# Dense stages of a two-block transformer kernel: waits by bank and by k step where there was one wait per stage

## The chip, the cores and the metric

The kernel runs on one core of a Trainium2 chip. The metric is the time of one execution on the device, in microseconds, taken as the median of several runs.

## The reference

All values are float32. The sequence has 256 tokens, the model width is 1024, the hidden width of the feed-forward parts 2816. The first block is

```python
x = x + 0.5 * swiglu(rms_norm(x, ffn1_norm[l]), ffn1_w_in[l], ffn1_w_out[l])
h = rms_norm(x, mix_norm[l])
p_rwkv, p_q, p_k, p_v, p_gate = _split_last(h @ w_in[l], ...)
y_a = rwkv7_time_mix(p_rwkv, ...)      # a scan over 256 tokens, 16 heads of 64
y_b = dilated_attention(p_q, p_k, p_v, ...)
g_a, g_b = _split_last(jax.nn.sigmoid(p_gate + b_gate[l]), (D_MODEL, D_MODEL))
merged = g_a * (y_a @ w_proj_rwkv[l]) + g_b * (y_b @ w_proj_attn[l])
x = x + merged @ w_out[l]
x = x + 0.5 * swiglu(rms_norm(x, ffn2_norm[l]), ffn2_w_in[l], ffn2_w_out[l])
```

The second has two layers over these 256 tokens and 256 context tokens; each layer is, in short,

```python
ul, uc = _split_cols(hl @ w_in), _split_cols(hc @ w_in)
ml_l, ml_c = _mlstm_branch(ul, uc, ml_gate_b, ml_head_g)
da_l, da_c = _diff_attn_branch(ul, uc, da_lam, da_head_g, cos, sin, lam_init, need_ctx)
fn_l, fn_c = _fourier(ul[8]), _fourier(uc[8])
gm, gd, gf = jnp.split(jax.nn.sigmoid(g_pre), N_BRANCH, axis=-1)
y = gm * (ym @ w_br_ml) + gd * (yd @ w_br_da) + gf * (yf @ w_br_fn)
x = x + gate * (y @ w_out)
x = x + gate2 * ((silu(a) * b) @ w_ffn_out)     # a, b = split(h @ w_ffn_in)
```

In the last layer the context tokens are needed only as keys and values, so most products have 256 columns there and 512 in the layer before (`nq`).

## The kernel before, in words

Activations lie transposed in SBUF: 8 tiles (`KT`) of 128 features by 256 or 512 tokens. Weights come from HBM in slabs of 2 MB (`SLAB`, 32 blocks of 128 x 128) or 1.4 MB (`DOWN`, 22 blocks) into a ring of three slots. SP issues them in the order of `stage_list`, each as soon as `tile_done` says that the slab three before it has been used.

A dense stage (`Stage`, a row of `stage_list`) is one or more slabs. `project` (line 530) makes four output tiles of each slab, one in each of PSUM banks 0 to 3, each with 8 matmuls over k. When a tile is complete, `tile_done` goes up; ScalarE (`act_out`) or VectorE (`dve_out`) evicts it. `by_act` and `by_dve` say whose eviction of bank c in slab j - 1 must be over before slab j writes that bank. `project_tokens` (line 553) is the same with tokens as output rows. Banks 4 to 7 serve norms, transposes and attention.

Between stages stands `enter` (line 520): it waits until all evictions of all stages before are done, both on `act_out` and `dve_out`.

The stages that matter here:

- `ffn` (line 603): eleven `up` slabs; ScalarE puts silu of banks 0 and 1 into a buffer, VectorE multiplies with banks 2 and 3 into `hid` (22 tiles). Then eight `down` slabs, each 22 matmuls over `hid` into banks 0, 1, 2 in turn, behind an `enter`.
- `rwkv_r`, `rwkv_k`, `rwkv_v`, `rwkv_lora_in`: ScalarE evicts with line 1279, and VectorE mixes each tile with its shifted self. `rwkv_lora_out` has 24 small tiles (lines 1300 to 1304). Two gate stages follow, and then the scan, between whose steps `ada_fill` places the 12 slabs of `ada0`, in bank 7.
- `merge` (line 629) does for each of two halves a gate stage (sigmoid by ScalarE, line 1260) and a projection stage, whose tiles VectorE multiplies with the gates and, but for the first branch, adds to the sum `G2` (lines 1657 and 1658). `mix_out` and `l0_out`, `l1_out` multiply that sum with the output weights. Before them VectorE says `dve_for_pe` by a one-element memset (`say`, line 1663).
- In each layer `ml_q`, `ml_k`, `ml_v` (evictions of lines 1488, 1489, 1491), attention, `ml_o`, merge, `da_q`, `da_k` (1507, 1508), each followed by `rotate` (line 1080), which multiplies the evicted tiles with a permutation into banks 4 to 7, `da_v` (1510), attention, merge, `fn` (1537), two Fourier products, merge, output stage, `ffn`.

`norm_sums` (line 592) adds the squares of 8 tiles by matmuls with ones, each behind its own wait. All matmuls are recorded at line 515, in `matmul`.

Of the kernel before, what the change touches and what calls it, by code (L numbers as in the profile page):

```python
# [18 lines left out]
P = 128  # L19
D = 1024  # L20
KT = D // P
T = 256
# [277 lines left out]
def program(nc, x_in, ctx_in, wide_in, down_in, par_in, const_in, const1_in, const2_in, out, dbg=None):  # L300
    with ExitStack() as ctx:
# [208 lines left out]
        def _(pe):  # L510
# [19 lines left out]
            def project(st, rhs, n, kt=KT, drains=None, part=(0, 4)):  # L530
# [22 lines left out]
            def project_tokens(st, lhs, n_tok, width, groups=4):  # L553

                enter(st)
                for j in range(st.slabs):
                    arrived(st, j)
                    for q in range(n_tok):
                        if j >= 1:
# [42 lines left out]

            def ffn(name, h, width):
# [3 lines left out]
                enter(st)  # L607

                def body(j, i):
                    arrived(st, j, i)  # L610
                    b = j % SLOTS
                    if j >= SLOTS:
                        pe.wait_ge(S["dve_out"], st.dve0 + j - SLOTS + 1 + i * SLOTS)
                    for k in range(FT):
                        last = matmul(bank[b][:, 0:width], wtile(st, j, k), hid[:, k], start=k == 0, stop=k == FT - 1)
                    last.then_inc(S["tile_done"], 1)

                over_slabs(pe, st.slabs, body, SLOTS)

            def gate(name, half, part=(0, 4)):  # L620

                project(ST[f"{name}_gate{half}"], lambda k: H1[:, k], T, drains=by_act, part=part)

            def branch_projections(name, y, kt=KT):
                t.wait("dve_for_pe")
                for half in range(2):
                    project(ST[f"{name}_proj{half}"], lambda k: y[:, k], T, kt=kt, drains=by_dve)

            def merge(name, h, y, width, kt=KT, output=None):
# [13 lines left out]
            for n in ("r", "k", "v"):  # L643
                project(ST["rwkv_" + n], lambda k: H1[:, k], T, drains=by_act)
            st = ST["rwkv_lora_in"]
            enter(st)
            arrived(st, 0)
            for c in range(3):
                for k in range(KT):
# [31 lines left out]
            gate("rwkv", 0)  # L681
            head_sums("dve_for_pe", "pe_for_dve")
            gate("rwkv", 1)
# [255 lines left out]
            project_tokens(ST["dil_v"], lambda k, q: H1[:, k, q * P:(q + 1) * P], 2, 384)  # L939
            branch_projections("rwkv", slot3(sR))  # L940
# [3 lines left out]
            for half in range(2):  # L944
# [8 lines left out]
                gate("dil", 0, part=(2 * half, 2 * half + 2))  # L953
# [38 lines left out]
            gate("dil", 1)  # L992
# [6 lines left out]
            branch_projections("dil", tiles(A, 0, 6, T), kt=6)  # L999
            pe.wait_ge(S["dve_out"], ST["mix_out"].dve0)  # L1000
            t.wait("dve_for_pe")
            project(ST["mix_out"], lambda k: G1[:, k], T, drains=by_dve)
# [5 lines left out]
            for la in range(2):  # L1008
# [13 lines left out]
                project(ST[p + "ml_k"], lambda k: H2[:, k], 2 * T, drains=by_act)  # L1022
                project_tokens(ST[p + "ml_v"], lambda k, q: H2[:, k, q * P:(q + 1) * P], 4, 512)
# [31 lines left out]
                pe.wait_ge(S["act_out"], ST[p + "ml_v"].act_end)  # L1055
                ml_shift_row(0, 0)
                for s in range(4):
                    ml_scores(0, s)
                ml_shift_row(0, 1)
# [16 lines left out]
                merge(p + "ml", H2, tiles(A, 0, KT, 2 * T), nq)  # L1076
# [13 lines left out]
                project(ST[p + "da_q"], lambda k: H2[:, k, 0:nq], nq, drains=by_act)  # L1090
                rotate("da_q", qT, True)
                project(ST[p + "da_k"], lambda k: H2[:, k], 2 * T, drains=by_act)
                rotate("da_k", kT, False)
                project_tokens(ST[p + "da_v"], lambda k, q: H2[:, k, q * P:(q + 1) * P], 4, 512)
                t.wait("dve_for_pe", 4)
                pe.wait_ge(S["act_out"], ST[p + "da_v"].act_end)
# [36 lines left out]
                for n in range(len(units) + 3):  # L1133
                    if n < len(units):
# [7 lines left out]
                merge(p + "da", H2, tiles(A, 0, KT, 2 * T), nq,  # L1142
                      output=lambda: token_outputs_back(t, transpose, 12288, qtiles, 8))

                project_tokens(ST[p + "fn"], lambda k, q: H2[:, k, q * P:(q + 1) * P], qtiles, 512)
                pe.wait_ge(S["act_out"], ST[p + "fn"].act_end)
# [5 lines left out]
                for k in range(KT):  # L1152
                    for s in range(nq // T):
# [18 lines left out]
                merge(p + "fn", H2, tiles(A, 0, KT, 2 * T), nq)  # L1172
                t.wait("dve_for_pe")
                project(ST[p + "out"], lambda k: G2[:, k, 0:nq], nq, drains=by_dve)
# [385 lines left out]
        def _(dve):  # L1560
# [393 lines left out]
            say("dve_for_pe")  # L1954
# [11 lines left out]
            for la in range(2):  # L1966
# [180 lines left out]
                say("dve_for_pe")  # L2147
# [217 lines left out]
```

## Time and profile before

| | |
|---|---|
| median of three runs | 3860.63 us (3856.47 to 3863.88) |
| profiled execution: its time, its span | 3863.46 us, 3861.7 us |
| busy TensorE | 3556.0 us (92%), 15308 matmul records |
| busy VectorE, ScalarE | 816.5 us (21%), 538.8 us (14%) |
| mean granted clock of TensorE | 0.956 |
| read from HBM | 368.84 MB, 96 GB/s |

The span runs from the first to the last instruction of the profiled execution. A float32 matmul of 128 x 128 weights is two records. A granted clock of 1 is 2.4 GHz, one of 0.5 is 1.2 GHz. In the rows, "idle before" is time in which the engine did nothing, and the arrow names what ended it; "issue" means that the profile shows nothing.

### The profile page before, as it was taken

The numbers are of one execution on the slowest core, as the hardware profiler recorded it, in microseconds if no ns is written. First come the engines' busy times: TensorE is split into PE (matmuls) and PEld (weight loads), VectorE is DVE, ScalarE is ACT, GpSimd is POOL, SyncE is SP. The second block draws the span as 40 slices with busy tenths as digits, with TensorE's granted clock in tenths as the row PEclk, the third lists the DMA queues.
The fourth block names the chain that finished last, engine by engine and source line by source line (L and its number), as shares of the span: only waits on it lengthen the run. The fifth ranks groups of instructions, "written<-read, shape, count | busy, mean of one in ns | idle before, by whom it ended". The sixth has DMA issues, their size and how long they took to land.

```text
span 3861.7 us, 35455 instructions
## 1 busy us (share of the span) xinstructions
PE 3556.0 (92%) x15308; PEld 2267.8 (59%) x15308; DVE 816.5 (21%) x1509; ACT 538.8 (14%) x1040; POOL 0.2 (0%) x4
## 2 busy tenths in 40 slices
PE   8998899799998989999799999999979899899898
PEld 7877687577873444444444444444434585467787
DVE  1012632521002053110830011000030421430101
ACT  1002221121002011000510101000021110311100
POOL 0000000000000000000000000000000000000000
PEclk9999899879999999999999998999989999999999
DMA  4343432224343200211012013121212132122332
GB/s 183 144 148 131 171 137 89 109 101 174 139 155 152 85 25 27 79 68 65 23 44 73 36 66 122 75 82 50 78 71 79 44 113 105 44 104 93 131 139 101
DMA packets 27501, 371.95 MB, mean 96 GB/s; under 512 B 3040, under 2 KB 3168, under 8 KB 3296
## 3 DMA queue, kind: packets, MB, share of 16 engines
q1 hardware_dynamic: 27216, 368.85, 25.9%
q8 instruction: 109, 1.79, 0.2%
q10 hardware_dynamic: 144, 1.05, 0.1%
q14 instruction: 32, 0.26, 0.0%
HBM read 368.84 MB, written 1.05 MB: 96 GB/s over the span
## 4 chain that ended last, share of the span: by engine, by line
PE 87%; DVE 9%; ACT 2%; issue 2%; DMA 0%; DVEq 0%; SPq 0%; ACTq 0%
PE bank L515 86%; DVE small L2110 1%; PE bank L518 1%; DVE merged_T L2048 1%; DVE arena L1903 1%; DVE merged_T L2062 1%; DVE arena L1579 0%; DVE arena L2082 0%; DVE h_T L1585 0%; DVE arena L1881 0%; DVE arena L2120 0%; DVE arena L2042 0%; DVE arena L2121 0%; DVE h_T L1606 0%; ACT L1198 0%
## 5 line engine op out<-in xcount | busy, mean ns | idle before, releaser
L515 PE MATMUL bank<-h_T,weights 128*128 128x256 f32 (+1 forms) x5744 | 1689.5, 457 | 52.3 <-DVE h_T L1585 16.8
L515 PEld LDWEIGHTS bank<-h_T,weights 128*128 128x128 f32 x5744 | 1100.7, 192 | 637.6 <-issue 493.3
L515 PE MATMUL bank<-arena,weights 128*128 128x256 f32 (+2 forms) x2464 | 713.0, 454 | 24.3 <-issue 6.4
L515 PEld LDWEIGHTS bank<-arena,weights 128*128 128x128 f32 (+1 forms) x2464 | 469.8, 194 | 266.9 <-issue 195.1
L515 PE MATMUL bank<-weights,h_T 128*128 128x512 f32 (+1 forms) x768 | 324.3, 584 | 4.2 <-issue 2.7
L515 PEld LDWEIGHTS bank<-weights,h_T 128*128 128x128 f32 x768 | 145.6, 190 | 181.3 <-issue 169.9
L515 PE MATMUL bank<-arena 64*64 64x64 f32 (+7 forms) x1616 | 220.9, 336 | 25.1 <-DVE arena L1905 8.6
L1625 DVE TENSOR_TENSOR arena<-arena,bank 128x256 f32 (+3 forms) x88 | 42.9, 488 | 726.4 <-PE bank L515 726.4
L515 PEld LDWEIGHTS bank<-arena 64*64 64x64 f32 (+2 forms) x1616 | 151.4, 178 | 67.8 <-issue 23.2
L1244 ACT ACTIVATE arena<-bank 128x256 f32<-128x256 f32 (+1 forms) x88 | 38.5, 437 | 664.2 <-PE bank L515 664.2
L515 PE MATMUL bank<-arena,merged_T 128*128 128x257 f32 (+1 forms) x528 | 91.7, 351 | 36.9 <-DVE merged_T L2062 19.9
L1657 DVE TENSOR_TENSOR arena<-arena,bank 128x256 f32<-128x256 f32 (+1 forms) x40 | 21.1, 528 | 460.6 <-PE bank L515 460.6
L515 PE MATMUL bank<-merged_T,weights 128*128 128x256 f32 (+1 forms) x384 | 110.9, 451 | 4.3 <-DVE small L1663 4.3
L515 PEld LDWEIGHTS bank<-arena,merged_T 128*128 128x128 f32 (+1 forms) x528 | 68.7, 192 | 59.8 <-DVE merged_T L2062 24.6
L515 PEld LDWEIGHTS bank<-merged_T,weights 128*128 128x128 f32 x384 | 72.7, 190 | 42.5 <-issue 30.1
L518 PE MATMUL bank<-common,arena 128*128 128x128 f32 x332 | 62.3, 319 | 29.0 <-DVE arena L2121 26.6
L515 PE MATMUL bank<-arena,common 128*128 128x512 f32 (+1 forms) x140 | 60.1, 569 | 27.9 <-ACT arena L1208 10.2
L518 PEld LDWEIGHTS bank<-common,arena 128*128 128x128 f32 x332 | 41.5, 160 | 73.6 <-DVE arena L2121 57.6
L2110 DVE TENSOR_REDUCE small<-bank 128x1 f32<-128x512 f32 (+1 forms) x96 | 57.8, 602 | 105.2 <-PE bank L515 102.0
L1260 ACT ACTIVATE arena<-bank 128x512 f32<-128x512 f32 (+1 forms) x48 | 23.5, 491 | 371.0 <-PE bank L515 370.9
L515 PE MATMUL bank<-arena,masks 128*128 128x256 f32 (+2 forms) x288 | 64.1, 375 | 5.0 <-ACT arena L1508 1.5
L515 PE MATMUL bank<-masks,arena 64*64 64x64 f32 (+1 forms) x704 | 62.9, 274 | 6.2 <-issue 4.7
(235 smaller groups left out, 1616.2 us busy)
## 6 DMA issues: line engine op xcount, KB each, us to landing
weights<-wide_slabs_dram SPq DMA_DIRECT2D x151, 2048.0 KB, 7.7
weights<-down_slabs_dram SPq DMA_DIRECT2D x32, 1408.0 KB, 5.8
masks<-second_consts_dram SPq DMA_DIRECT2D x1, 2240.0 KB, 8.8
masks<-first_consts_dram SPq DMA_DIRECT2D x1, 1120.0 KB, 7.5
x_T<-x_T_dram SPq DMA_DIRECT2D x1, 1024.0 KB, 4.9
merged_T<-ctx_T_dram SPq DMA_DIRECT2D x1, 1024.0 KB, 10.9
out_dram<-h_T ACTq DMA_DIRECT2D x1, 1024.0 KB, 3.9
params<-params_dram SPq DMA_DIRECT2D x1, 287.5 KB, 5.2
```

The lines of the kernel that those rows point to most:

```text
L515: return mm(out, lhsT, rhs, start=start, stop=stop, skip_group_check=True)
L518: return nc.tensor.transpose(out, in_, ident[0:in_.shape[0], 0:in_.shape[0]])
L1244: af(tmp[:, c], bank[c][:, 0:width], ACT.Silu).then_inc(S["silu_ready"], 1)
L1260: tiles_of(st, lambda c, j, i: af(gt[:, c, 0:width], bank[c][:, 0:width], ACT.Sigmoid))
L1625: tt(dst, tmp[:, c], bank[2 + c][:, 0:width], mul).then_inc(S["dve_out"], 1)
L1657: t.step(tt(gt[:, c, 0:width], gt[:, c, 0:width], bank[c][:, 0:width], mul))
L1903: t.step(nc.vector.reciprocal(rs, rs))
L2048: t.out(stt(at, bank[d][:, 0:nq], ML_COLS[:, 0, s, d, h:h + 1], C[:, m0:m0 + nq], add, ALU.min), "ml_args")
L2062: t.out(tt(at, at, bank[4 + s][:, 0:nq], mul), "ml_weights")
L2110: t.step(nc.vector.tensor_reduce(sc[:, m:m + 1], bank[4 * m + n % 2][:, 0:w], axis=AX.X, op=ALU.max))
```

## The change

`enter` is dropped at most stages. `project` and `project_tokens` take a list `frees` instead: for bank c the semaphore and the count that its last reader reaches; `take` waits for it in front of the first tile in that bank. `act_frees(name)` and `dve_frees(name)` give the last four evictions of a stage. Where the operands are made by the stage just before, the wait for them is per k step: `summed=True` for `mix_out` and the layers' output stages (whose `say` on VectorE goes away), and the first slab of each down stage. `rotate`, the first attention scores behind `da_v`, the use of `ml_v` and the first Fourier product wait for the tiles they read. The `enter` of `ada0` moves behind its first six steps.

```diff
+            def act_frees(name, n=4):
+                return [("act_out", ST[name].act_end - n + 1 + c) for c in range(n)]
+
+            def dve_frees(name, n=4):
+                return [("dve_out", ST[name].dve_end - n + 1 + c) for c in range(n)]
+
+            def take(frees, c):
+                name, count = frees[min(c, len(frees) - 1)]
+                pe.wait_ge(S[name], count)
+
+            def project(st, rhs, n, kt=KT, drains=None, part=(0, 4), frees=None, summed=False):
+                if frees is None:
+                    enter(st)
...
+                        elif frees is not None:
+                            take(frees, c)
                         for k in range(kt):
+                            if summed and j == 0 and c == part[0]:
+                                pe.wait_ge(S["dve_out"], st.dve0 - kt + 1 + k)
...
             def ffn(name, h, width):
...
-                enter(st)
+                silus[0] += FT
...
+                    if j == 0:
+                        pe.wait_ge(S["silu_ready"], silus[0] - 1)
                     for k in range(FT):
+                        if j == 0:
+                            pe.wait_ge(S["dve_out"], st.dve0 - FT + 1 + k)
...
+            def merge(name, h, y, width, frees, kt=KT, output=None):
                 for half in range(2):
-                    project(ST[f"{name}_gate{half}"], lambda k: h[:, k, 0:width], width, drains=by_act)
+                    gate_st = f"{name}_gate{half}"
+                    project(ST[gate_st], lambda k: h[:, k, 0:width], width, drains=by_act,
+                            frees=frees if half == 0 else dve_frees(name + "_proj0"))
...
-                    project(ST[f"{name}_proj{half}"], lambda k: y[:, k, 0:width], width, kt=kt, drains=by_dve)
+                    project(ST[f"{name}_proj{half}"], lambda k: y[:, k, 0:width], width, kt=kt, drains=by_dve, frees=act_frees(gate_st))
...
             pe.wait_ge(S["cond_ready"], 1)
-            enter(ada_st)
             for _ in range(6):
                 ada_fill()
+            enter(ada_st)
...
                 def rotate(name, src, first):
-                    pe.wait_ge(S["act_out"], ST[p + name].act_end)
                     for n in range(4):
+                        pe.wait_ge(S["act_out"], ST[p + name].act0 + 2 * n + 2)
...
-                pe.wait_ge(S["act_out"], ST[p + "da_v"].act_end)
...
                 for n in range(len(units) + 3):
+                    if n < 4:
+                        take(act_frees(p + "da_v"), n)
...
-                t.wait("dve_for_pe")
-                project(ST[p + "out"], lambda k: G2[:, k, 0:nq], nq, drains=by_dve)
+                project(ST[p + "out"], lambda k: G2[:, k, 0:nq], nq, drains=by_dve, frees=dve_frees(p + "fn_proj1"), summed=True)
...
@@ -2144,7 +2168,6 @@
                 merge(p + "fn", G2, nq, False)
-                say("dve_for_pe")
```

The stages that are left out of this diff (`rwkv_k`, `rwkv_v`, `rwkv_lora_in`, the gates and projections of the first block, `ml_k`, `ml_v`, `da_q`, `da_k`, `da_v`, `fn`) get their `frees` in the same way. `ffn`'s up stages, `rwkv_r`, `rwkv_lora_out`, `dil_qk`, `ml_q` and `ml_o` keep `enter`.

## Rows read from the trace of the kernel before

**Rows 1.** the page: shares of the chain that ended last, by engine

```profile
PE 87%; DVE 9%; ACT 2%; issue 2%; DMA 0%; DVEq 0%; SPq 0%; ACTq 0%
```

**Rows 2.** waits of TensorE, whole span: total us, times, longest us

```profile
PE bank L515 <- DVE small L1663: 38.6, 7, 21.6
PE bank L515 <- issue: 29.4, 29, 2.4
...
PE bank L515 <- ACT arena L1488: 6.4, 3, 5.1
...
PE bank L515 <- ACT arena L1260: 3.8, 6, 0.7
...
PE bank L515 <- ACT arena L1510: 1.7, 2, 0.8
PE bank L515 <- ACT arena L1489: 1.5, 2, 0.7
PE bank L515 <- ACT arena L1537: 1.5, 2, 0.7
PE bank L515 <- ACT arena L1508: 1.5, 2, 0.7
...
PE bank L515 <- ACT x_T L1279: 1.4, 3, 0.5
PE bank L515 <- ACT arena L1507: 1.3, 2, 0.7
...
PE bank L515 <- DVE arena L1625: 0.5, 1, 0.5
PE bank L515 <- ACT arena L1304: 0.5, 1, 0.5
```

**Rows 3.** timeline of TensorE, first block: start, us, instructions, idle before

```profile
254.58 3.62 PE L515 MATMUL bank<-merged_T,common 128*128 128x256 f32 x16
...
296.55 27.89 PE L515 MATMUL bank<-h_T,weights 128*128 128x256 f32 x128 [0.47 <-ACT x_T L1279]
...
440.24 1.92 PE L515 MATMUL bank<-weights,conditions 128*32 128x512 f32 x16 [0.61 <-issue]
...
708.18 14.05 PE L515 MATMUL bank<-arena,weights 128*128 128x256 f32 x64 [0.63 <-issue]
...
849.26 10.60 PE L515 MATMUL bank<-arena,weights 128*128 128x256 f32 x48 [1.09 <-issue]
861.10 27.86 PE L515 MATMUL bank<-merged_T,weights 128*128 128x256 f32 x128 [1.24 <-DVE small L1663]
```

**Rows 4.** timeline of TensorE, the two layers

```profile
1261.78 55.20 PE L515 MATMUL bank<-h_T,weights 128*128 128x512 f32 x128 [0.75 <-ACT arena L1488]
...
2007.42 27.70 PE L515 MATMUL bank<-h_T,weights 128*128 128x512 f32 x64 [1.62 <-issue]
...
2293.93 55.17 PE L515 MATMUL bank<-merged_T,weights 128*128 128x512 f32 x128 [1.78 <-DVE small L1663]
...
2684.30 151.30 PE L515 MATMUL bank<-arena,weights 128*128 128x512 f32 x352 [0.83 <-issue]
...
3768.86 76.21 PE L515 MATMUL bank<-arena,weights 128*128 128x256 f32 x352 [0.56 <-issue]
```

**Rows 5.** waits of TensorE, stretches 1570:1840, 2000:2300, 3135:3333, 3420:3575

```profile
PE bank L515 <- issue: 2.6, 3, 0.9
...
PE bank L515 <- issue: 5.7, 4, 1.6
...
PE bank L515 <- issue: 1.8, 3, 0.6
...
PE bank L515 <- issue: 3.9, 4, 1.1
```

**Rows 6.** the page: one group of weight loads; busy, mean ns, idle

```profile
L515 PEld LDWEIGHTS bank<-merged_T,weights 128*128 128x128 f32 x384 | 72.7, 190 | 42.5 <-issue 30.1
```

**Rows 7.** windows, one stretch: busy of PE, PEld, DVE, ACT, POOL, granted clock, DMA

```profile
2178.00:2348.00 170.00, 164.95 (x382) 72.36 (x383) 17.85 (x31) 9.24 (x16) 0.00 (x0) 1.00 0.17 62
```

More of the change, by code:

```diff
@@ L551, in _, with project_tokens @@
             by_pairs = [("dve_out", c % 2) for c in range(4)]
-            def project_tokens(st, lhs, n_tok, width, groups=4):
-                enter(st)
+            def project_tokens(st, lhs, n_tok, width, frees):
                 for j in range(st.slabs):
@@ L618, in ffn, with gate, branch_projections @@
                 over_slabs(pe, st.slabs, body, SLOTS)
-            def gate(name, half, part=(0, 4)):
-                project(ST[f"{name}_gate{half}"], lambda k: H1[:, k], T, drains=by_act, part=part)
-            def branch_projections(name, y, kt=KT):
+            def gate(name, half, frees, part=(0, 4)):
+                project(ST[f"{name}_gate{half}"], lambda k: H1[:, k], T, drains=by_act, part=part, frees=frees)
+            def branch_projections(name, y, frees, kt=KT):
                 t.wait("dve_for_pe")
                 for half in range(2):
-                    project(ST[f"{name}_proj{half}"], lambda k: y[:, k], T, kt=kt, drains=by_dve)
-            def merge(name, h, y, width, kt=KT, output=None):
+                    project(ST[f"{name}_proj{half}"], lambda k: y[:, k], T, kt=kt, drains=by_dve,
+                            frees=frees if half == 0 else dve_frees(name + "_proj0"))
+            def merge(name, h, y, width, frees, kt=KT, output=None):
                 for half in range(2):
-                    project(ST[f"{name}_gate{half}"], lambda k: h[:, k, 0:width], width, drains=by_act)
+                    gate_st = f"{name}_gate{half}"
+                    project(ST[gate_st], lambda k: h[:, k, 0:width], width, drains=by_act,
+                            frees=frees if half == 0 else dve_frees(name + "_proj0"))
                     if half == 0:
@@ L642, in _ @@
             norm_sums(T, G)
-            for n in ("r", "k", "v"):
-                project(ST["rwkv_" + n], lambda k: H1[:, k], T, drains=by_act)
+            for n, frees in (("r", None), ("k", act_frees("rwkv_r")), ("v", act_frees("rwkv_k"))):
+                project(ST["rwkv_" + n], lambda k: H1[:, k], T, drains=by_act, frees=frees)
             st = ST["rwkv_lora_in"]
-            enter(st)
             arrived(st, 0)
             for c in range(3):
+                take(act_frees("rwkv_v"), c)
                 for k in range(KT):
@@ L952, in _ @@
                 last.then_inc(S["pe_for_dve"], 1)
-                gate("dil", 0, part=(2 * half, 2 * half + 2))
+                gate("dil", 0, dve_frees("rwkv_proj1"), part=(2 * half, 2 * half + 2))
             t.wait("dve_for_pe")
@@ L991, in _ @@
             t.wait("pv_out", 2)
-            gate("dil", 1)
+            gate("dil", 1, act_frees("dil_gate0"))
             t.wait("dve_for_pe")
@@ L998, in _ @@
             last.then_inc(S["pe_for_dve"], 1)
-            branch_projections("dil", tiles(A, 0, 6, T), kt=6)
-            pe.wait_ge(S["dve_out"], ST["mix_out"].dve0)
-            t.wait("dve_for_pe")
-            project(ST["mix_out"], lambda k: G1[:, k], T, drains=by_dve)
+            branch_projections("dil", tiles(A, 0, 6, T), act_frees("dil_gate1"), kt=6)
+            project(ST["mix_out"], lambda k: G1[:, k], T, drains=by_dve, frees=dve_frees("dil_proj1"), summed=True)
             norm_sums(T, A, ada="ada1a")
@@ L1053, in ml_values @@
                         last.then_inc(S["pv_psum"], 1)
-                pe.wait_ge(S["act_out"], ST[p + "ml_v"].act_end)
+                take(act_frees(p + "ml_v"), 0)
                 ml_shift_row(0, 0)
@@ L1058, in _ @@
                     ml_scores(0, s)
+                take(act_frees(p + "ml_v"), 3)
                 ml_shift_row(0, 1)
@@ L1141, in _ @@
                 t.wait("pv_out", 2)
-                merge(p + "da", H2, tiles(A, 0, KT, 2 * T), nq,
+                merge(p + "da", H2, tiles(A, 0, KT, 2 * T), nq, act_frees(p + "da_v"),
                       output=lambda: token_outputs_back(t, transpose, 12288, qtiles, 8))
-                project_tokens(ST[p + "fn"], lambda k, q: H2[:, k, q * P:(q + 1) * P], qtiles, 512)
-                pe.wait_ge(S["act_out"], ST[p + "fn"].act_end)
+                project_tokens(ST[p + "fn"], lambda k, q: H2[:, k, q * P:(q + 1) * P], qtiles, 512, dve_frees(p + "da_proj1"))
                 z = tiles(A, 4096, 4, D)
@@ L1171, in _ @@
                 t.wait("act_for_pe", 4)
-                merge(p + "fn", H2, tiles(A, 0, KT, 2 * T), nq)
-                t.wait("dve_for_pe")
-                project(ST[p + "out"], lambda k: G2[:, k, 0:nq], nq, drains=by_dve)
+                merge(p + "fn", H2, tiles(A, 0, KT, 2 * T), nq, act_frees(p + "fn", qtiles))
+                project(ST[p + "out"], lambda k: G2[:, k, 0:nq], nq, drains=by_dve, frees=dve_frees(p + "fn_proj1"), summed=True)
                 norm_sums(nq, A, signals=KT * nq // T, ada="ada1c" if la == 0 else None)
```

30 lines of the change are left out of this document (16 added, 14 removed).

## The prediction, made before the changed kernel was run

> **What bounds the kernel now.** The chain that ended last comes first: 87% of it is TensorE, 9% VectorE, and no step of it is a transfer [rows 1]. So a microsecond off TensorE's stream counts, unless what stands behind it hangs on another engine's older work. The weight slabs are no such thing: no part of the chain is DMA.
>
> Next come TensorE's waits over the whole span [rows 2]. The reader is to see two kinds. A few are long (up to 21.6 us) and end on a result of VectorE or ScalarE that the next matmul really needs; the change leaves them. Many are short and alike, 0.5 to 0.7 us each: lines 1260, 1279, 1304, 1488, 1489, 1507, 1508, 1510, 1537 are ScalarE's evictions, line 1625 is VectorE's last product before a down stage. Those put down to "issue" are partly the same thing: the profile names no releaser, but the timeline shows them at stage starts behind a VectorE eviction, 0.63 us where it is one operation of 256 columns, 1.09 where it is two [rows 3], 1.62 at 512 columns [rows 4].
>
> Then the timeline at each stage start. Each float32 matmul shows as two records. A stage of 128 records is one unbroken piece, though it holds a wait for each bank of its second slab; the break comes only where `enter` (line 520) waits for the last bank of the stage before, while the new stage's first bank has been free for three banks' time [rows 3, 4].
>
> **What the change removes.** I go through the stages in order, and count a gap only if every wait that ends it is loosened.
>
> ScalarE and VectorE by name [rows 2]: line 1260 (gate to projection of the second half) 3.8 us in 6 gaps; 1510 (first attention scores behind `da_v`) 1.7 in 2; 1489, 1537 and 1508 4.5 in 6; 1279 (`rwkv_r`, `k`, `v` to the next) 1.4 in 3; 1507 1.3 in 2; 1625 and 1304 1.0 in 2; 1488 6.4 less its longest of 5.1, which is a wait inside `ml_q` and stays: 1.3 in 2. Together 15.0 us, 23 gaps.
>
> "Issue": inside the two layers' merge stages 2.6 + 5.7 + 1.8 + 3.9 = 14.0 us in 14 gaps [rows 5]. Outside them the start of `ada0` 0.61, `rwkv_proj1` 0.63, `dil_proj1` 1.09 [rows 3], the down stages 0.83 and 0.56 [rows 4], and that of `ffn2`, the same edit at the same width, 0.56. Together 18.3 us in 20 gaps. The other nine of the 29 "issue" waits lie inside the scan or behind `pv_out`, and stay.
>
> The output stages wait for `say` (line 1663): 1.24 at `mix_out` [rows 3], 1.78 at `l0_out` [rows 4], `l1_out` has the width of `mix_out` and counts the same. Together 4.3 us in 3 gaps; the other 34 us of that line are needed results and stay.
>
> Sum: 37.6 us in 46 gaps. Each break costs more than its idle time, since the last matmul before it drains with nothing behind it. At 256 columns, 64 records take 14.05 and 128 take 27.89 [rows 3]: 0.216 each, so the last one is 14.05 - 63 x 0.216 = 0.43 long, 0.21 beyond its pitch. At 512 columns, 27.70 and 55.20 [rows 4]: 0.430 each, the last 0.63, again 0.20. 46 x 0.20 = 9.4 us (rounded up from 9.2 for the 256-column ones). In all 47 us.
>
> **Does the gap go, or shrink?** What replaces it must be ready earlier than it is asked for. By banks: bank 3 is wanted 3 x 16 records later, 10 us at 256 columns and 20 at 512, and was free after at most 1.62. By k steps: `mix_out` wants its eighth operand after 14 records, 3.0 us, where the whole wait was 1.24; `l0_out` after 6.0 us against 1.78; a down stage its 22nd after 42 records, 9.1 us against 0.56 and 18 against 0.83; `rotate` its last pair after 12 records, 2.6 us against 0.75. So all of them go to nothing. Down stages also wait for `silu_ready` less one: the gate tile of bank 0, read well before the last up tile ends.
>
> **Where the work behind does not hang on TensorE.** After `da_v` come scores, VectorE's maxima, ScalarE's exponentials, in a chain that begins with the scores; it moves up whole. ScalarE's last eviction of `da_v` now runs beside the first scores, and takes less than they do. Before the scan, VectorE's chain starts from the last eviction of `lora_out`, and the gate stages are beside it; there 0.47 and 0.61 are the two gaps that could be absorbed, 1.5 us with their drains. The long waits that are left keep their length, since each is measured from a TensorE release that moves with the rest.
>
> **What the change adds.** About 350 waits are put in (some 200 `take`, 88 + 24 for k steps, 4 each of `silu_ready` and others) and some 120 taken out. They cost nothing if a satisfied wait lets the weight load run ahead. The trace has that case: a norm's sums, eight matmuls with a wait before each, run behind a down stage as 16 records in 3.62 us without idle time [rows 3], 0.213 each; the unbroken pitch is 0.216. The bound below is 0. Above, I allow 0.02 us a wait, what these rows could hide, 7 us for 350. I take 0, as that row is the very pattern. The Trainium skill ("Advanced Engine Details and Errata", Network/Comms) puts reading a semaphore from the sequencer at 50 to 100 ns. By that, an estimate, 230 more waits would be 12 to 23 us if none were hidden, and the sum 24 to 35 instead of 47; the sums' row speaks against it.
>
> `ada0`'s `enter` moves behind six fills. These use bank 7 and the modulation tiles alone, and they have their own wait for `ada_free`; the moved wait is long satisfied there.
>
> SP waits for `tile_done`, which comes earlier, so slabs are fetched earlier; nothing waits for them.
>
> **Sum.** The profiled execution took 3863.5 us around a span of 3861.7. 3863.5 - 47 = 3816.5. The median of the runs is 2.8 us below the profiled one, so I predict a median of 3814. On a median of 3861, 0.2% is 7.7 us; that is about what the runs can tell from no change.
>
> **Rivals.**
>
> 1. *Waits are not free* (the other side: slower). If a satisfied wait keeps the next weight load from running ahead, each costs a load of 0.19 us [rows 6]; 350 x 0.19 = 66 us against 47: 3880. It decides from 47 / 350 = 0.13 us a wait. For it: the k waits sit between matmuls with 0.43 us from one to the next, where the queue has little lead. Against it: the sums' row. 3%.
>
> 2. *Waits cost a little, or the change does only part*: a quarter of a weight load for each wait, 0.05 us, or the drain of 0.2 not given back because the first load behind a wait is late, or the gains ahead of the scan and of the attentions taken up by VectorE. Any of these is 8 to 20 us less: 3822 to 3834. For it: 'issue' gaps name no releaser, and I assigned them from the code. 14%.
>
> 3. *The clock gives back more.* The granted clock is 0.956 over the span, so there is something to gain. Against it: the stretch 2178 to 2348 holds four of the gaps, up to 1.78 us, and has clock 1.00 [rows 7]; the short gaps do not lower it. The half-speed stretches follow the long waits, which stay, though they fall elsewhere by chance. The missing 0.044 of 3862 us is 170 us; a twentieth of it back is 8.5 us, 3805. The Trainium skill ("TensorE: Matmul & The Clock Gate", A second HAM failure mode) says that short idles between groups, from cycling through banks, can make the clock oscillate; by that rule the change would gain this too, but the row shows no oscillation to cure. 8%.
>
> 4. *No change*: another engine's chain is the true bound and the gaps reappear in front of the long waits. The 87% of TensorE speaks against it. 3861, 3%.
>
> The forecast itself, 3807 to 3821: 72%. Rivals 1 to 4 take the rest. The range reaches over most of 2 and 3: 3804 to 3829. Faster by over 0.2% (below 3853) are the forecast, 2 and 3: 94%; within it, rival 4 and a weak form of 1: 3%; slower 3%.
>
> **What the next profile would show.** Right: the span near 3815; in TensorE's waits the rows of lines 1260, 1279, 1304, 1489, 1507, 1508, 1510, 1537 and 1625 gone, line 1488 with its 5.1 alone, "issue" near 11 us in 9, line 1663 near 34 in 4. TensorE's busy time falls by the drains, 9 us, from 3556 to about 3547; if it stays, the drains were not given back. A norm's sums still take 3.62; a down stage still takes 76.2 and 151.3 for its 352 records. If these have grown, waits are not free. Wrong: short gaps that stand at the same places with another releaser, or the long waits of VectorE's chains longer by what the stages before them gained.

## The result, and the profile after

The changed kernel takes 3816.14 us (median of four runs, 3813.28 to 3819.17), the kernel before 3862.24 in the runs beside it (3856.47 to 3863.88). The ratio is 0.9883, with a 95% interval from 0.9872 to 0.9895: 1.2% faster, 46 us. The prediction said 3814. The profiled execution took 3813.28 us against 3863.46 before, 50.2 us less.

The page of the changed kernel, the lines for the span, the busy times and the chain's shares by engine, shows what to expect of a kernel that lost waits and no work:

```profile
span 3811.4 us, 35451 instructions
...
PE 3546.8 (93%) x15308; PEld 2270.4 (60%) x15308; DVE 816.2 (21%) x1506; ACT 538.8 (14%) x1040; POOL 0.2 (0%) x4
...
PE 87%; DVE 9%; ACT 2%; issue 1%; DMA 0%; DVEq 0%; SPq 0%; ACTq 0%
```

TensorE has the same 15308 records and is busy 9.2 us less (3556.0 before); its idle time, span less busy, went from 305.7 to 264.6, 41.1 us less. These two make the 50 us. The chain is made of the same engines, and only its share of "issue" changed, from 2% to 1% [rows 1].

TensorE's waits over the whole span of the changed kernel (total us, times, longest us). The change shifts line numbers by 25: 1663 is now 1688, 1488 is 1513.

```profile
PE bank L515 <- DVE small L1688: 34.3, 4, 21.6
...
PE bank L515 <- issue: 9.2, 9, 2.4
...
PE bank L515 <- ACT arena L1513: 5.1, 1, 5.1
...
PE bank L515 <- ACT arena L1568: 1.5, 2, 0.7
PE bank L515 <- ACT arena L1573: 1.3, 2, 0.7
```

Against [rows 2]: every short wait that the prediction named is gone, "issue" went from 29 waits to 9, and the long ones kept their length (21.6, 5.1). The last two rows are the waits around the second Fourier product, which the change doesn't touch.

The timeline of TensorE in the changed kernel (start, us, instructions, idle before) has no bracket where the rows of before had a short wait (the 8.39 and 2.49 are long ones that stay):

```profile
255.57 3.62 PE L515 MATMUL bank<-merged_T,common 128*128 128x256 f32 x16
267.58 95.78 PE L515 MATMUL bank<-h_T,weights 128*128 128x256 f32 x432 [8.39 <-DVE h_T L1610]
...
829.78 20.99 PE L515 MATMUL bank<-arena,weights 128*128 128x256 f32 x96 [2.49 <-DVE arena L1973]
850.60 27.79 PE L515 MATMUL bank<-merged_T,weights 128*128 128x256 f32 x128
...
1199.30 110.03 PE L515 MATMUL bank<-h_T,weights 128*128 128x512 f32 x256
1309.17 55.10 PE L515 MATMUL bank<-weights,h_T 128*128 128x512 f32 x128
...
2181.75 27.63 PE L515 MATMUL bank<-arena,weights 128*128 128x512 f32 x64
2209.21 27.63 PE L515 MATMUL bank<-h_T,weights 128*128 128x512 f32 x64
2236.68 27.63 PE L515 MATMUL bank<-arena,weights 128*128 128x512 f32 x64
2264.15 55.10 PE L515 MATMUL bank<-merged_T,weights 128*128 128x512 f32 x128
...
2650.98 151.23 PE L515 MATMUL bank<-arena,weights 128*128 128x512 f32 x352
...
3718.66 76.14 PE L515 MATMUL bank<-arena,weights 128*128 128x256 f32 x352
```

`rwkv_r` to `rwkv_lora_in` are one piece of 432 records, `ml_q` and `ml_k` one of 256, and the down stages follow on their up stages without a break, in 151.23 and 76.14 where they took 151.30 and 76.21 [rows 4]: the 23 waits in front of their first slab cost nothing. A norm's sums take 3.62, as before [rows 3].

### The profile page after: what moved, and what is told of

It reads as the page before. It is cut to its first block, busy times and chain, and to the rows that moved or that the text cites. A ratio compares the mean times of both kernels' runs of the same rounds, so it can differ in the third digit from the quotient of the medians.

```text
span 3811.4 us, 35451 instructions
## 1 busy us (share of the span) xinstructions
PE 3546.8 (93%) x15308; PEld 2270.4 (60%) x15308; DVE 816.2 (21%) x1506; ACT 538.8 (14%) x1040; POOL 0.2 (0%) x4
## 4 chain that ended last, share of the span: by engine, by line
PE 87%; DVE 9%; ACT 2%; issue 1%; DMA 0%; DVEq 0%; SPq 0%; ACTq 0%
PE bank L515 87%; DVE small L2134 1%; PE bank L518 1%; DVE merged_T L2072 1%; DVE merged_T L2086 1%; DVE arena L1928 1%; DVE arena L1604 0%; DVE arena L2106 0%; DVE h_T L1610 0%; DVE arena L1906 0%; DVE arena L2144 0%; DVE arena L2145 0%; DVE arena L2066 0%; DVE h_T L1631 0%; ACT L1223 0%
## 5 line engine op out<-in xcount | busy, mean ns | idle before, releaser
L515 PE MATMUL bank<-arena,merged_T 128*128 128x257 f32 (+1 forms) x528 | 86.7, 332 | 36.5 <-DVE merged_T L2086 19.5
L1543 ACT ACTIVATE arena<-bank,small 128x512 f32<-128x512 f32 (+1 forms) x96 | 59.1, 616 | 61.1 <-DVE small L2135 59.5
```

The source lines that it names most:

```text
L515: return mm(out, lhsT, rhs, start=start, stop=stop, skip_group_check=True)
L1543: ins = af(DA_P(n, m)[:, 0:w], bank[4 * m + n % 2][:, 0:w], ACT.Exp, scale=0.125, bias=sc[:, m:m + 1], accum_out=sc[:, 2 + m:3 + m])
```

## The experiments

Each line of code is against the changed kernel unless said otherwise. Ratios are to the kernel before, run on the same chip.

### The waits per k step, undone

```diff
-                if frees is None:
+                if frees is None or summed:
                     enter(st)
...
-                            if summed and j == 0 and c == part[0]:
-                                pe.wait_ge(S["dve_out"], st.dve0 - kt + 1 + k)
...
                 silus[0] += FT
+                enter(st)
...
-                    if j == 0:
-                        pe.wait_ge(S["silu_ready"], silus[0] - 1)
...
-                        if j == 0:
-                            pe.wait_ge(S["dve_out"], st.dve0 - FT + 1 + k)
```

> The changed kernel with its waits per k step undone: the four down stages, mix_out and the layers' two output stages begin behind enter again (without the say of VectorE). Own theory: only these seven gaps come back. Their idle times before were 0.51, 0.56, 0.83, 0.56, 1.24, 1.78 and 1.25 us, 6.7 together, and each costs 0.27 us more for the restart, so 8.6 us over the changed kernel: 3825 us where that takes 3816. In TensorE's waits, one row for each of the seven, and no others new. Rival (waits are not free): 112 k waits fewer, so if a satisfied wait costs 0.1 us or more, this kernel is no slower than the changed one.

Measured: 3820.35 us (3816.64 to 3823.24), ratio 0.9893 (0.9878 to 0.9908). From its waits and its timeline:

```profile
PE bank L515 <- issue: 15.9, 15, 2.0
...
2662.37 151.31 PE L515 MATMUL bank<-arena,weights 128*128 128x512 f32 x352 [0.83 <-issue]
...
3727.66 76.21 PE L515 MATMUL bank<-arena,weights 128*128 128x256 f32 x352 [0.56 <-issue]
```

"Issue" has six more waits and 6.7 us more, and a seventh is back by its name, 0.5 us in front of a down stage. 0.83 and 0.56 are the very values of [rows 4]. Of the 6.7 us the six hold 5.8; the rest is in "issue" waits inside the scan, which differ from trace to trace. So the seven gaps brought 6.3 us of idle time back (6.7 were expected), about 8 with their restarts. The profiled executions, both at a mean clock of 0.954, are 9.0 us apart (3822.26 and 3813.28), but the medians differ by 4 us with overlapping intervals: the 3825 that was expected was missed, and the time alone would not have told this part; the trace does.

### The waits by bank, all on the last bank

```diff
             def take(frees, c):
-                name, count = frees[min(c, len(frees) - 1)]
+                name, count = frees[-1]
                 pe.wait_ge(S[name], count)
```

> The changed kernel in which take waits for the last entry of its list for each bank, so that every dense stage again waits for the last bank of the stage before, by the same number of waits as the changed kernel; k steps, rotate and the first Fourier product stay loosened. Own theory: the wait for the last bank is what cost, not how it is written: 28 us of idle time in 33 gaps come back, 37 us with the restarts, 3853 us. Rival (number and kind of waits matter, or the gain came from the order of ada0 or the k steps): under half of it, below 3835.

Measured: 3852.86 us (11 runs, 3847.13 to 3861.21), ratio 0.9979 (0.997 to 0.9988). `enter` is still gone here and as many waits are issued as in the changed kernel; they only name a later eviction. That gives back nearly 37 of the 46 us, as expected: 30.4 us of idle time and 9.3 of TensorE's busy time in the trace. Its waits and its timeline in the first layer's last merge, to be read beside the rows 2181.75 to 2264.15 above:

```profile
PE bank L515 <- DVE merged_T L1683: 9.5, 7, 1.7
...
PE bank L515 <- ACT arena L1285: 7.3, 10, 0.8
...
PE bank L515 <- DVE merged_T L1680: 3.9, 5, 0.9
```

```profile
2206.37 27.70 PE L515 MATMUL bank<-arena,weights 128*128 128x512 f32 x64 [0.84 <-ACT arena L1285]
2235.74 27.70 PE L515 MATMUL bank<-h_T,weights 128*128 128x512 f32 x64 [1.67 <-DVE merged_T L1683]
2264.28 27.71 PE L515 MATMUL bank<-arena,weights 128*128 128x512 f32 x64 [0.84 <-ACT arena L1285]
```

This settles what the profile of before could not say. There the breaks in the merges were put down to "issue" [rows 5]; with a wait that names one eviction, the same breaks at the same places carry the name of VectorE's product or ScalarE's sigmoid. They were evictions all along, as the prediction had assigned them from the code. Three breaks keep the name "issue" here, those in front of `mix_out`, `l0_out` and `l1_out` (1.09, 1.62 and 1.09 us), where the waits per k step stand beside the one for the eviction.

### A satisfied wait before each dense matmul, and two

```diff
+                            pe.wait_ge(S["loads"], 64)
                             last = matmul(bank[c][:, 0:n], wtile(st, j, c * kt + k), rhs(k), start=k == 0, stop=k == kt - 1)
```

The same line stands before the matmuls of `project_tokens` and of the down stages: 4,624 waits more, on a semaphore that has long reached its value. The second kernel adds `pe.wait_ge(S["landed0"], 16)` to each, 9,248 in all.

> The changed kernel with one more wait, long satisfied (for the first loads), in front of each of the 4,624 dense matmuls. Own theory: nothing, 3816 us, and a down stage of 352 records still takes 76.1 us at 256 columns. Rival (a satisfied wait holds back the next weight load, 0.19 us each): 880 us more. A cost of 0.02 us, the bound of the prediction, would be 92 us more.

> As the run before, with two satisfied waits, on two semaphores, in front of each dense matmul, so that many matmuls have a third. Own theory: nothing as long as the matmul before (0.43 us at 256 columns) covers them, 3816 us; if two or three waits can't ride on one instruction and each extra one takes an instruction of its own in TensorE's queue, it is still hidden, or costs up to 0.05 us each, 230 us. Rival as before: 1760 us more.

Measured: 3811.05 us (3809.02 to 3816.71), ratio 0.9873 (0.9858 to 0.9889) with one; 3813.03 (3808.36 to 3816.38), ratio 0.9876 (0.9861 to 0.9891) with two. The down stages of the first and the second:

```profile
2649.78 151.23 PE L515 MATMUL bank<-arena,weights 128*128 128x512 f32 x352
...
3717.44 76.14 PE L515 MATMUL bank<-arena,weights 128*128 128x256 f32 x352
```

```profile
2649.41 151.23 PE L515 MATMUL bank<-arena,weights 128*128 128x512 f32 x352
...
3717.06 76.14 PE L515 MATMUL bank<-arena,weights 128*128 128x256 f32 x352
```

To the hundredth the times of the changed kernel, with 176 and 352 waits more in each stage; `ml_q` and `ml_k` of the first layer take 110.03 us in all three kernels. A satisfied wait in front of a dense matmul costs nothing here, and the rival *Waits are not free* is out. The Trainium skill ("Advanced Engine Details and Errata", Network/Comms) gives 50 to 100 ns for reading a semaphore from the sequencer; by that, an estimate, 4,624 would be 231 to 462 us if they lay on the path. No part of it shows: if it is spent, it is hidden. The names in the profile did change: the 5.1 us inside `ml_q` of the second layer, line 1513 in the changed kernel, are 5.04 us of "issue" with one more satisfied wait behind the one that counts. That both kernels are some 3 to 5 us below the changed one isn't explained, and with overlapping intervals may be nothing.

### The changed kernel again, and the four waits it left in the Fourier products

The changed kernel ran again, for its own scatter beside the next kernels; it is the same code.

> The changed kernel once more, beside the kernels that add to it, for comparison on one chip. Both theories: 3816 us.

Measured: 3815.78 us (3812.1 to 3819.2), ratio 0.9885 (0.987 to 0.99).

The next kernel gives the second Fourier product the same treatment:

```diff
-                t.wait("act_for_pe", 4)
                 for k in range(KT):
...
-                    if k >= 4:
-                        t.wait("act_for_pe")
+                    t.wait("act_for_pe")
...
-                t.wait("act_for_pe", 4)
-                merge(p + "fn", H2, tiles(A, 0, KT, 2 * T), nq, act_frees(p + "fn", qtiles))
+                merge(p + "fn", H2, tiles(A, 0, KT, 2 * T), nq, act_frees(p + "fn", qtiles),
+                      output=lambda: t.wait("act_for_pe", 4))
```

> The changed kernel with the same edit at the two places where its trace still shows short waits for an eviction (lines 1568 and 1573, 1.5 and 1.3 us in two gaps each): the second Fourier product waits bank by bank for the first, and the wait for its own evictions moves behind the gate stage that follows. Own theory: these 2.8 us go, and 4 x 0.27 us of restarts, 3.9 us: 3812 us. Rival: their time goes into a longer wait behind, no change; within the spread, so the four gaps in TensorE's waits decide.

Measured: 3816.85 us (3812.8 to 3825.74), ratio 0.9893 (0.9878 to 0.9908): no gain. Its timeline shows that the waits themselves went:

```profile
2096.20 27.63 PE L515 MATMUL bank<-masks,arena 128*128 128x512 f32 x64
2123.66 27.63 PE L515 MATMUL bank<-arena,masks 128*128 128x512 f32 x64
2151.13 27.63 PE L515 MATMUL bank<-h_T,weights 128*128 128x512 f32 x64
```

The changed kernel, run beside it, at the same place:

```profile
2101.60 27.63 PE L515 MATMUL bank<-masks,arena 128*128 128x512 f32 x64
2129.98 27.73 PE L515 MATMUL bank<-arena,masks 128*128 128x512 f32 x64 [0.75 <-ACT arena L1568]
2158.46 27.73 PE L515 MATMUL bank<-h_T,weights 128*128 128x512 f32 x64 [0.75 <-ACT arena L1573]
```

From the start of the first group to that of the third it is 56.86 us with the waits and 54.93 without: the two waits are gone whole, 1.9 us. But the mean granted clock of this kernel's runs was 0.952, 0.949, 0.950 and 0.951, that of the changed kernel beside it 0.955, 0.954, 0.952 and 0.952. Within one kernel, runs with a mean clock lower by 0.001 are 3 to 5 us longer (the kernel with all waits on the last bank: 3847.13 us at 0.955, 3861.21 at 0.952). A clock lower by 0.002 or 0.003 is more than the four waits were worth. So my expectation, 4 us, failed by something other than the rival I had named, and a gain of this size cannot be told from no change in this kernel. Why the clock came lower is open.

### The long waits: the first stage behind a norm

What remains of TensorE's idle time is long waits. A norm signals `h_ready` once when all 8 normalised tiles are written, and TensorE waits for all. On top of the Fourier kernel:

```diff
+                            if normed and j == 0 and c == part[0]:
+                                pe.wait_ge(S["h_ready"], normed[0] + normed[1] * (k + 1))
...
-                    ins = stt(h[:, k], x[:, k, 0:width], pc(gain, k), r, mul, mul)
-                    if k < KT - 1:
-                        t.step(ins)
-                t.out(ins, "h_ready")
+                    t.out(stt(h[:, k], x[:, k, 0:width], pc(gain, k), r, mul, mul), "h_ready")
```

> The run before, and the first stage behind a norm waits for each normalised tile instead of all eight (ffn1, rwkv_r, ffn2, both layers' ffn). Own theory: VectorE makes these tiles at 0.52 us each and TensorE uses one in 0.43, so the three idle times of 8.4, 8.4 and 8.9 us (ffn1, rwkv_r, the last layer's ffn) shrink by 7 tiles, about 3 to 3.6 us each: 10 us less, 3802 us. The other two norms are covered by modulation work and give nothing. Rival: matmuls with gaps between them keep the clock at 1.2 GHz for longer, and the stages' first slab gives 2 us of each back: 3808.

Measured: 3807.21 us (3797.31 to 3811.44), ratio 0.9864 (0.9849 to 0.9879). In its timeline:

```profile
258.29 95.52 PE L515 MATMUL bank<-h_T,weights 128*128 128x256 f32 x432 [4.84 <-DVE h_T L1611]
```

4.84 us of idle time where it was 8.39, and likewise 3.5 us less at two more norms; 9.6 us off the median of the Fourier kernel. The four runs spread over 14 us, with mean clocks from 0.954 down to 0.951, so the 10.6 us of idle time in the trace are the firmer figure. The expectation of 3802 rested on the changed kernel less both steps; the 5 us missing are those of the kernel before.

### `ml_q` into the longest wait

The 21.6 and 8.3 us of line 1688 lie in front of the gate product that opens a layer, which waits for VectorE to fold the gate weights, while `ml_q` behind it needs only the normed tiles. On top of the last kernel:

```diff
+                project(ST[p + "ml_q"], lambda k: H2[:, k, 0:nq], nq, drains=by_act, normed=normed)
...
                 last.then_inc(S["pe_for_act"], 1)
-                project(ST[p + "ml_q"], lambda k: H2[:, k, 0:nq], nq, drains=by_act)
...
+                tiles_of(ST[p + "ml_q"], lambda c, j, i: af(qT[:, 4 * j + c, 0:nq], bank[c][:, 0:nq], ACT.Copy))
                 t.wait("pe_for_act")
```

> The run before, and in each layer ml_q runs ahead of the gate product that waits for VectorE's memsets (on ScalarE its evictions too). Own theory: the idle times of 8.3 and 21.6 us before the gate product and the 5.1 us inside ml_q of the last layer are filled: 8 us in the first layer; in the last one TensorE starts 22 us earlier and the stage after ml_q begins 19 us earlier. 27 us less than the run before, 3775 us. Rival: the chain of the gates (ScalarE's logarithms, VectorE's scans) starts 14 us later and delays the first attention: the gain falls to 10 us, 3792.

Measured: 3780.54 us (3777.61 to 3782.92), ratio 0.979 (0.9777 to 0.9803), and again, beside the kernels of the next part:

> The kernel of e8_q_first once more, beside e9 on the same chip: 3780 us under both theories.

3780.0 us (3774.38 to 3780.78), ratio 0.9788 (0.9773 to 0.9802). The first run's waits and its timeline in the two layers:

```profile
PE bank L515 <- ACT h_T L1248: 14.1, 4, 8.0
...
PE bank L515 <- DVE small L1685: 4.4, 2, 2.6
```

```profile
1183.07 55.18 PE L515 MATMUL bank<-h_T,weights 128*128 128x512 f32 x128
1238.09 7.03 PE L515 MATMUL bank<-h_T,merged_T 128*128 128x512 f32 x16
...
2814.23 5.82 PE L515 MATMUL bank<-h_T,weights 128*128 128x256 f32 x12 [7.99 <-ACT h_T L1248]
```

The 34.3 us of that line became 4.4. In the first layer nothing is idle in front of `ml_q`; in the second the norm itself is late, and 8.0 of the 21.6 us stay under its name. Net 27 us, the larger part of what all short waits together gave, by one stage moved.

### What the clock gives when the waits are filled

The same kernel, with matmuls in the long waits whose results nothing reads; they are no part of the reference's work.

```diff
+            def fill(n, b):
+                for _ in range(n):
+                    matmul(bank[b][:, 0:T], ones, com[:, 0:T])
...
                     ada_group(ada)
+                fill(filled, 5)
...
+            ffn("ffn1", H1, T, norm_sums(T, A, filled=6))
+            normed = norm_sums(T, G, filled=6)
...
                 gate("dil", 0, dve_frees("rwkv_proj1"), part=(2 * half, 2 * half + 2))
+                fill(14, 7)
```

The second layer's two norms get 14 and 6.

> The kernel of the run e8_q_first, with matmuls that nobody reads put into five of TensorE's longest waits (128x256 on constants into a free bank: 6 each behind the sums of ffn1, rwkv_r and the last layer's ffn, 14 in the last layer's first norm, 14 behind each of the two dil_gate0 parts). They are sized to end before the wait does. This adds work to the computation and takes none away. Own theory on the clock: it falls where TensorE has been idle for some microseconds, and the stage behind then runs its first 3 to 7 us at 1.2 GHz; busy waits keep it at 2.4 GHz, so about six half-speed stretches go, the mean granted clock rises by 0.01 and the time falls by 1.5 to 3 us each, 10 us: 3770 against 3780. Rival: the placement of half-speed stretches has nothing to do with these waits; then the clock stays at 0.954 and the time is the same or up to 5 us longer, as the filler itself is in the way.

Measured: 3765.91 us (3755.53 to 3770.33), ratio 0.9754 (0.9735 to 0.9772), 14 us below the kernel without fills run beside it. Span and mean granted clock, first of this one, then of the one without:

```profile
core 0: 3763.6 us, clock 0.962
```

```profile
core 0: 3779.0 us, clock 0.954
```

Then each half of the fills alone.

> The kernel that filled TensorE's waits, with the 28 unread matmuls between the parts of the first attention's gate stage taken out: left are those behind the norms' sums (6, 6, 14 and 6). Their work is not part of the result. Theory (the fill behind the sums of the second norm keeps the clock up in what follows, the scan among it): most of the 14 us is here, about 3769, mean granted clock 0.960. Rival (each filled wait gives back only its own half-speed stretch, in equal parts): about 3773. Rival (no filled wait matters by itself, the order of the stretches is chance): anywhere from 3766 to 3780.

> The other part alone: the 28 unread matmuls in the first attention's gate stage, none behind the norms' sums. Theory: the scan lies ahead of this place and keeps its half-speed stretches; about 3776, mean granted clock 0.956, and the stretch 430 to 680 has the clock 0.93 that it had without any filling. Rival (equal parts): about 3773. Rival (chance): 3766 to 3780, and the clock of 430 to 680 may be 0.97 though nothing ahead of it has changed.

Measured: behind the norms' sums alone 3767.77 us (3764.61 to 3770.92), ratio 0.9757 (0.9744 to 0.977), mean clock 0.958 to 0.960; in the gate stage alone 3776.59 us (3772.36 to 3779.8), ratio 0.9779 (0.9766 to 0.9792), 0.956 to 0.959. By the ratios that is 12 us below the kernel without fills (0.9757 against 0.9788) with the norms' fills and 3 to 4 with the gate stage's (0.9779, whose interval overlaps), as the theory had it. The windows of the stretch with the scan (stretch, its length, busy of PE, PEld, DVE, ACT and POOL, granted clock, DMA share, GB/s), in this order of kernels: no fills, the gate stage's, the norms':

```profile
430.00:680.00 250.00, 229.36 (x4012) 188.82 (x4004) 86.56 (x123) 57.18 (x92) 0.00 (x0) 0.93 0.39 145
```

```profile
430.00:680.00 250.00, 227.47 (x4023) 185.69 (x4022) 90.02 (x126) 60.93 (x95) 0.00 (x0) 0.95 0.41 148
```

```profile
430.00:680.00 250.00, 228.37 (x4039) 187.69 (x4032) 90.45 (x127) 60.56 (x95) 0.00 (x0) 0.97 0.42 153
```

The clock of this stretch rises from 0.93 to 0.97 with the fills ahead of it. But it is 0.95 with the gate stage's fills too, which lie behind the scan and can't have changed it. Measured by the work instead, from the 54 records of `rwkv_lora_out` to the first part of `dil_gate0`, the scan took 344.6 us without fills, 335.8 with the gate stage's, 334.2 with the norms' and 334.4 with all. In the kernels without any fill it took anything from 335.5 to 344.6, and the changed kernel alone has 335.7 in one profiled execution and 342.3 in the other. So all but 1 to 2 us of the 10 that the scan gave here have come without any filling as well.

What the fills do next to themselves is small. Behind the second norm (255 to 290 us) the granted clock is 0.90 in the four kernels with this norm loosened and no fill, and 1.00 in the two with one; the 432 records there take 94.0 us instead of 95.5 to 95.8. In the last layer's `ffn` a fill gave 0.2 us. In the 100 us from the first part of `dil_gate0` on, the clock is 0.62 without and 0.69 with fills, but the stages up to the next gate take 90.9 and 91.4 us where they took 91.7 to 92.7 without. At `ffn1` nothing shows. Together that is 2 to 4 us of the 14.

So it is shown that the medians fell, with times and mean clocks that don't overlap (0.958 to 0.960 in five runs with the norms' fills, 0.953 to 0.957 in ten without any), and that a fill can cure the half-speed stretch next to it. That the larger part, in the scan, comes from the fills is not shown: every kernel here is another program, and the scan's clock changes from program to program, and from run to run, without them.

The version with all fills and that with the norms' alone are the fastest of all kernels here, 2.5% and 2.4% below the kernel before; their intervals overlap.

## Why the prediction was right

**The bound.** TensorE's stream set the end, and the 46 gaps removed from it moved the end by their whole length, 49.0 us by the sum below in 50.2. No long wait grew: 21.6 us [rows 2] is still 21.6. *No change* is out.

**Which gaps.** All that were named went, and 29 "issue" waits became 9, the count that was forecast; that the 20 were evictions was an assignment from the code, and the kernel with all waits on the last bank shows it. They held 18.2 us by the timeline of before, where 18.3 had been summed. The total of "issue" fell by 2.0 us more (29.4 less 9.2 is 20.2), since the six waits inside the scan that stay held 9.7 us before and 7.7 after. Another 1.7 us of idle time went at line 1214 (now 1239), 27.3 before and 25.6 after, and they are no gain: in front of the second modulation step of `ada0` a group of 16 records took 3.61 us where it had taken 1.92, and the wait behind it 2.35 where it had been 4.04. TensorE was slower there and waited less by the same 1.69. With these the 37.6 us that were named make the 41.1.

**The restart, the term that was mis-sized.** I took 0.20 us for each gap beyond its idle time, the drain of the last matmul. The traces give 0.23 to 0.28. Two groups of before follow on the first of [rows 4] and on the second of [rows 3]:

```profile
324.92 27.89 PE L515 MATMUL bank<-h_T,weights 128*128 128x256 f32 x128 [0.47 <-ACT x_T L1279]
...
1317.73 55.20 PE L515 MATMUL bank<-weights,h_T 128*128 128x512 f32 x128 [0.75 <-ACT arena L1489]
```

At 512 columns the start-to-start time was 1317.73 - 1261.78 = 55.95 us for 128 records; after the change two such stages take 1309.17 - 1199.30 = 109.87, 54.94 each. 1.01 less for a gap of 0.75. At 256 columns it was 324.92 - 296.55 = 28.37, and after the change

```profile
3102.44 13.98 PE L515 MATMUL bank<-arena,weights 128*128 128x256 f32 x64
3116.25 13.98 PE L515 MATMUL bank<-h_T,weights 128*128 128x256 f32 x64
3130.06 13.98 PE L515 MATMUL bank<-arena,weights 128*128 128x256 f32 x64
```

13.81 for 64, so 27.62: 0.75 less for a gap of 0.47, 0.28. The part missed is at the start. A group of 64 at 512 columns takes 27.63 us without a wait ahead, at a pitch of 27.47: its last record is 0.16 longer than the pitch. Behind a wait it takes 27.73 (the changed kernel's row at 2129.98) or 27.70 [rows 4]: its first record is longer too, by 0.10 or 0.07. The prediction took its pitch as the difference of two groups, 55.20 and 27.70, of which one had the 0.10 and the other the 0.07; that made the pitch 27.50 and lost most of the slower start. With 0.25 in the middle, 46 gaps are 11.5 us instead of 9.4.

**The sum.** 37.5 us of idle time in the 46 gaps and 11.5 of restarts make 49.0; the two profiled executions differ by 50.2. The 1.2 us between them are not assigned. TensorE's busy time fell by 9.2 and not by 11.5, so 2.3 us of work at the lower clock came in, net (mean clock 0.954 after, 0.956 before). The forecast of 3547 for it was met for that reason, and not because 0.20 was right. One place shows how far the clock can move: the windows of the modulation steps in front of the first layer, before and after (columns as above).

```profile
1158.00:1188.50 30.50, 19.48 (x145) 9.25 (x144) 11.97 (x23) 11.79 (x22) 0.00 (x0) 0.89 0.72 283
```

```profile
1144.80:1182.60 37.80, 27.22 (x145) 12.24 (x144) 11.67 (x21) 11.79 (x22) 0.00 (x0) 0.64 0.73 263
```

The same 145 records took TensorE 27.2 us where they had taken 19.5, at a clock of 0.64 against 0.89, with no edit there. Other places went the other way. The scan took 342.3 us before and 335.7 after, where the three gaps in it explain 2.5; two groups of modulation behind the first layer took 1.84 us each before (at 2371.62 and 2377.84) and 1.02 after (at 2341.71 and 2345.40).

The medians moved by 46 us and not by 50, and that is a second error of the prediction. It took 2.8 us off for the way from the profiled execution to the median, as in the kernel before. In the changed kernel the profiled execution was the fastest of the four, 2.9 below their median: 3813.28 where 3816.5 was forecast, and a median of 3816.14 where it was 3814. A gain a few us too small and an offset with the wrong sign nearly cancelled; that the forecast of the median is off by only 2 us is in part luck.

**Do the gaps go to nothing.** Yes: no short wait took the place of one removed, at any of the widths, and neither did one at the k steps, where the cover was thinnest (2.6 and 3.0 us). One short wait is new, 0.62 us in front of the first layer's `ffn`, where the edit changes nothing; the modulation groups just ahead of it are those that ran faster this time. Nor was anything absorbed ahead of the scan, which the prediction had left open: from the sums of the second norm to ScalarE's first exponential of the scan (line 1357, now 1382) it was 189.55 us before and is 186.76.

**The clock.** That short gaps don't lower it held: with the waits on the last bank, groups of 64 behind 0.84 to 1.67 us of idle time ran in 27.70 us, against 27.63 without gaps, and the granted clock from 2170 to 2300 us was 1.00 in that kernel. The Trainium skill ("TensorE: Matmul & The Clock Gate", A second HAM failure mode) describes, for a bf16 kernel, a clock that oscillates from small idles between groups; these rows show none. The rival *The clock gives back more* went the other way by a little. That the long waits are tied to the lost clock, which the prediction took from where the half-speed stretches lay, is borne out by the fills next to themselves; for most of what they gave it is open.

## What to carry to other kernels

A wait for "everything before" costs its idle time and a quarter of a microsecond of restart, each time; a wait for the one bank or tile that is touched costs nothing if it comes satisfied, so in front of float32 matmuls of 256 or 512 columns, the only ones tried here, it can be put before each operand without counting. When the profile puts a gap down to "issue", let the one wait in front of the matmul name one event: the same gap then mostly carries its cause. With a second wait beside it the name is lost again. Before polishing short waits look at what stands behind the longest one and does not need its result: one stage moved there gave 27 us where 46 short gaps gave 46. And where the clock is in question, compare the same work between two landmarks, in more than one kernel, before a gain is put down to an edit.

## What the runs showed of the hardware that was not expected

- 9,248 satisfied waits more, two before each dense matmul, change no dense stage that was compared by 0.01 us (151.23, 76.14 and 110.03 us with and without them).
- The restart behind a wait has two ends: 0.16 us of the last record before it and 0.07 to 0.10 of the first behind it at 512 float32 columns; 0.28 in sum in the one pair of groups at 256.
- The mean granted clock of one kernel differs from run to run (0.952 to 0.955 in 11 runs) and 0.001 of it is 3 to 5 us. A saving of 4 us was lost in it.
- With unread matmuls in long waits the mean clock was 0.962 instead of 0.954 and the time 14 us shorter, though they add work. Only 2 to 4 us of it lie next to the filled waits.
- The same work of the scan took from 335.5 to 344.6 us from program to program, and 335.7 and 342.3 in two executions of one program.
- A group at half speed can eat into the wait behind it and cost nothing: 1.69 us longer, and the wait 1.69 us shorter.
